# The last expert pair of a mixture-of-experts kernel: down blocks loaded in halves, and unread matrix products between its steps

## Chip, cores and metric

The kernel runs on one core of a Trainium2 chip. The metric is the device time of one execution in microseconds (us), as the median of several runs.

## The reference

Two transformer-like blocks are computed on 512 tokens of width 1024, in float32. The first block ends with an expert layer: 16 experts, each of which picks 64 tokens.

```
cap = EC_CAPACITY * t // N_EXPERTS                     # 2 * 512 // 16 = 64
aff = softmax(einsum('btd,de->bte', h, w_router))
gate, idx = top_k(swapaxes(aff, 1, 2), cap)
xs = h[idx]                                            # 64 tokens for each expert
hid = silu(einsum('becd,edf->becf', xs, w_gate)) * einsum('becd,edf->becf', xs, w_up)
ys = einsum('becf,efd->becd', hid, w_down) * gate
x = x + g2 * zeros.at[idx].add(ys)
```

For one expert w_gate and w_up are 1024x2048 and w_down is 2048x1024, 8 MB each; over 16 experts that is some 400 MB. The second block (attention, convolution, a wide feed-forward layer) works on the result of the first.

## The kernel before

Each engine has its own instruction list, written out by hand, and the lists meet only in semaphores. `sync` is the list of the queue that starts the loads (SP), `tensor` that of TensorE.

The experts are taken in 8 pairs (`p` from 0 to 7). One product computes 64 tokens of the first expert in one half of TensorE's columns, the next product the second expert's in the other half (`o[64 * e:64 * e + 64]`). A pair has 12 steps, 4 for the gate matrices, 4 for the up matrices (`expert_up`, kind 0 and 1) and 4 for the down matrices (the `k` loop from L1219), and each step reads one 2 MB block of each expert. So there are 24 blocks a pair and 192 in all (`NBLK`), number n = 24p + 8 kind + 2k + e for gate and up, 24p + 16 + 2k + e for down. The blocks lie in slots of SBUF that are used in turn; `sync` waits until TensorE has done with what a slot held before, and then starts the load (L565).

A down step has four row groups (`r`), each of four products: two column halves (`f`) by two experts (`e`). In the profile every float32 product is two MATMUL records, so a whole down step is 32 records and half of one is 16. Ahead of its products a step waits for its two blocks (`landed_block`, L1114) and for its transposed hidden values (`hT`). These are made by `turn_h` (L1154): four transposes on TensorE into a bank of PSUM, and a copy out of it by ScalarE (L1592). For pair 7 `turn_h` for steps 0 and 1 stands right behind the up steps, that for steps 2 and 3 in the middle of steps 1 and 2.

For pair 7 the last blocks are loaded in pieces: the blocks of down step 2 (n = 188, 189) as two halves of 1 MB, those of step 3 (n = 190, 191) as a half and two quarters. The first halves of the two experts come first and the later pieces after them, the two experts' in turn. The later pieces have semaphores of their own (`mg`, `mh`, `mq`), for which TensorE waits in front of the row group that reads them (L1225). The blocks of steps 0 and 1 (n = 184 to 187) are whole loads.

Behind the last down step the results are copied out of PSUM (ScalarE and VectorE), `combine` (L1105) adds them into the token rows by a product for each of 8 parts, and the first matrix of the second block is multiplied (L1286 to L1292), one part after each `combine`.

An earlier place of the kernel, the routing, has products whose result nobody reads: `keep_busy` (L1033), each an identity matrix by 256 columns of ones.

Of the kernel before, what the change touches and what calls it, by code (L numbers as in the profile page):

```python
# [17 lines left out]
NEG = -1e30  # L18

DMA_SEMS = (*(f"g{i}" for i in range(6)), *(f"cg{i}" for i in range(4)), *(f"zf{i}" for i in range(4)), "x0", "x1", "rows0", "rows", "small", "ctx", "wple", *(f"scale{i}" for i in range(4)), *(f"shift{i}" for i in range(4)), "w0", "w1", "ptok", "gf", "out",  # L20
            *(f"m{i}" for i in range(9)), "mx", "my", "mz", "rows2", "mg0", "mg1", "mh0", "mh1", "mq0", "mq1")
SEMS = (
    "hi", "lo_v", "pe_gla",
    "pe_pre", "pe_ada", "pe_proj", "pe_scores", "pe_scan", "pe_inter", "pe_fill", "pe_mix", "pe_route", "pe_gather",
# [20 lines left out]
def build_program(nc, I, out):  # L45
    ctx = ExitStack()
    with ctx:
        s = {n: ctx.enter_context(nc.semaphore("s_" + n)) for n in DMA_SEMS + SEMS}
# [5 lines left out]
        def up(ins, name, *key):  # L54
            ins.then_inc(s[name], 1)
            count[name] = at[(name, *key)] = at[name] = count.get(name, 0) + 1
# [19 lines left out]
        banks = [ctx.enter_context(nc.psum_tensor(f"bank{i}", [P, 512], F32)) for i in range(8)]  # L76
# [39 lines left out]
        ident = mem(128)  # L116
        onesD = mem(128)
        onesC = mem(128)
        ones256 = mem(256)
# [60 lines left out]
        NBLK = 192  # L180
# [8 lines left out]
        for n in range(NBLK):  # L189
# [10 lines left out]
            i = SLOT_OF[n] = turn_of[0]  # L200
# [45 lines left out]
        mx, sm = small[:, 96:128], small[:, 144:176]  # L246
# [196 lines left out]
        def sync(sp):  # L443
# [68 lines left out]
            for n in (0, 1, 2, 5, 7, 15, 3, 4, 6, 8, 22, *range(9, 15), *range(16, 22), *range(23, NBLK)):  # L512
                if n == 0:
                    sp.wait_ge(s["pe_inter"], val("pe_inter", 1, 3))
                if n == 1:
                    sp.wait_ge(s["a_fill"], val("a_fill"))
                    sp.wait_ge(s["v_fill"], val("v_fill"))
                    sp.wait_ge(s["g_y"], val("g_y"))
                r, src = n % 24, block(n)
                k = (r - 16) // 2  # L520
                if n == 15:
                    sp.wait_ge(s["pe_mix"], val("pe_mix", "xr", 3, 1))
                    sp.dma_start(once_x, src).then_inc(s["mx"], 16)
                    continue
                if n == 7:
                    sp.wait_ge(s["v_mix"], val("v_mix", "on", 3))
                    sp.dma_start(once_y, src[:, 0:2560]).then_inc(s["my"], 16)
                    continue
                if n == 8:
                    sp.dma_start(once_z, block(7)[:, 2560:3584]).then_inc(s["my"], 16)  # L530
                    sp.dma_start(once_s, block(7)[:, 3584:4096]).then_inc(s["my"], 16)
                if n == 22:
                    sp.wait_ge(s["pe_sq"], val("pe_sq", 1, 7, 0))
                    for place, c0, c1 in ((late_c, 0, 2048), (late_g, 2048, 3584), (late_y, 3584, 4096)):
                        sp.dma_start(place, src[:, c0:c1]).then_inc(s["mz"], 16)
                    continue
                if n in HALVED:
                    for half, z in enumerate((slice(0, 2048), slice(2048, 4096))):
                        for m in HALVES.get(n, ()):
                            used = moe_used(BEFORE[m]) if half else half_used(BEFORE[m])  # L540
                            sp.wait_ge(s[used[0]], val(*used))
                            sp.dma_start(moe_slot[SLOT_OF[m]][:, z], block(m)[:, z]).then_inc(s[f"m{SLOT_OF[m]}"], 16)
                    continue
                if n == 99:
                    sp.wait_ge(s["pe_down"], val("pe_down", 0, 3))
                    for dst, name in ((W2k, "w_cmp_k2_2"), (W2v, "w_cmp_v2_2")):
                        sp.dma_start(dst, I[name][0].rearrange("(k p) n -> p k n", p=P)).then_inc(s["rows2"], 16)
                    used = moe_used(before_ple)
                    sp.wait_ge(s[used[0]], val(*used))
                    sp.dma_start(ptok, I["p_2"][0, 0].rearrange("(t p) d -> p t d", p=P)).then_inc(s["ptok"], 16)  # L550
                    sp.dma_start(ple, I["w_ple_2"][0].rearrange("(k p) n -> p k n", p=P)).then_inc(s["wple"], 16)
                i = SLOT_OF[n]
                if BEFORE[n] is not None:
                    used = moe_used(BEFORE[n])
                    sp.wait_ge(s[used[0]], val(*used))
                elif n == 9:
                    sp.wait_ge(s["pe_route"], val("pe_route", "h2", 3, 1))
                elif n == 3:
                    sp.wait_ge(s["pe_mix"], val("pe_mix", "res", 3))
                elif n == 5:  # L560
                    sp.wait_ge(s["pe_mix"], val("pe_mix", "o", 3))
                elif n == 6:
                    sp.wait_ge(s["pe_mix"], val("pe_mix", "res", 7))
                if n < NBLK - 4:
                    sp.dma_start(moe_slot[i], src).then_inc(s[f"m{i}"], 16)  # L565
                    continue

                sp.dma_start(moe_slot[i][:, 0:2048], src[:, 0:2048]).then_inc(s[f"m{i}"], 16)
                if r % 2:
                    for name, c0, c1 in (("mg", 2048, 4096),) if k == 2 else (("mh", 2048, 3072), ("mq", 3072, 4096)):  # L570
                        for e_ in range(2):
                            src = I["w_down"][0, 14 + e_][512 * k:512 * k + 512, :].rearrange("(p r) n -> p (r n)", p=P)
                            sp.dma_start(moe_slot[SLOT_OF[n - 1 + e_]][:, c0:c1], src[:, c0:c1]).then_inc(s[f"{name}{e_}"], 16)
# [48 lines left out]
        def tensor(pe):  # L622
# [3 lines left out]
            def after(b):  # L626
                if b in free:
                    pe.wait_ge(s[free[b][0]], val(*free[b]))
# [525 lines left out]
            def turn_h(p, fc):  # L1154
                o = take(("hT", p, fc), "hT", p, fc)
                pe.wait_ge(s["v_up"], val("v_up", p, fc))
                up(turn_blocks(o, [ab[:, 512 * fc + 128 * j:512 * fc + 128 * j + 128] for j in range(4)]), "pe_up", "h", p, fc)
# [15 lines left out]
            def ple_product(n):  # L1173
# [6 lines left out]
                                    start=k == 0, stop=k == 1)  # L1180
                up(ins, "pe_ple", "e", n)

            turn["order"], turn["i"] = [6, 7, 4, 5], 0
            gather(0, 0)
            gather(0, 1)
            for p in range(8):
# [14 lines left out]
                for k in range(4):  # L1201
                    if p < 7 and 0 < k < 3:
                        expert_up(p, 1, k, (gather, p + 1, 2 * k - 2))
                        gather(p + 1, 2 * k - 1)
                    else:
                        expert_up(p, 1, k)
                    if p == 5:
                        ple_product(k)
                if 1 < p < 7:
# [9 lines left out]
                for k in range(4):  # L1219
                    ws = [landed_block(24 * p + 16 + 2 * k + e) for e in range(2)]  # L1220
                    pe.wait_ge(s["hT"], val("hT", p, k))
                    for r in range(4):
                        for f in range(2):
                            for e in range(2):
                                if p == 7 and f == 0 and (k, r) in ((2, 2), (3, 2), (3, 3)):  # L1225
                                    pe.wait_ge(s[f"{'mg' if k == 2 else 'mh' if r == 2 else 'mq'}{e}"], 16)
                                ins = pe.matmul(o[f][64 * e:64 * e + 64, :], hT[:, 4 * k + r, 64 * e:64 * e + 64],  # L1227
                                                ws[e](1024 * r + 512 * f), start=k + r == 0, stop=k == 3 and r == 3)
                        if r == 1 and p == 0:
                            up(ins, "pe_half", 2, k)  # L1230
                        if r == 1 and k < 3 and (p < 7 or k):
                            turn_h(p, k + 1)
                    up(ins, "pe_down", p, k)
                    for k_ in later.get(k, ()):
                        gather(p + 1, k_)
                    if p == 4 and k < 2:
                        ple_turned(k)
                    if p == 5:
                        ple_product(4 + k)
                    if p == 1:  # L1240
                        turn_back(2 * k)
                        turn_back(2 * k + 1)
                        combine(0, 2 * k)
                        combine(0, 2 * k + 1)
# [52 lines left out]
            for j in range(4):  # L1297
                if j == 1:
                    for name, row in (("rr", 0), ("r1", 32)):
# [3 lines left out]
                                     start=True, stop=True), "pe_z", name)  # L1303
# [243 lines left out]
            for h in range(2):  # L1547
                os_ = [take(("dn", 4 * h + j), "xt", "dn", 4 * h + j) for j in range(4)]
                for i, (k0, nk) in enumerate(KD):
                    c = DN + 3 * h + i  # L1550
                    wh, wl = tiles(c, nk)
                    for k in range(nk):
                        kk = k0 + k
                        n = 22 * h + kk
# [1594 lines left out]
```

## Time and profile before

| | |
|---|---|
| median of 3 runs | 2057.58 us (2056.42 to 2061.18) |
| profiled execution, its own time | 2058.38 us |
| its span, first to last instruction | 2056.7 us |
| TensorE busy in the span | 1982.4 us, 96% |
| VectorE / ScalarE busy | 889.0 us / 578.2 us |
| DMA, mean over the span | 257 GB/s |
| chain that ended last | TensorE 94%, issue 2%, VectorE 2%, DMA 1%, ScalarE 1% |

The span is less than the execution's own time because what lies before the first and after the last instruction is not in it. Times inside the trace count from the span's start. The granted clock is the share of TensorE's full clock that the chip let through: 1.00 is 2.4 GHz, 0.50 is 1.2 GHz.

### The profile page before, as it was taken

What the parts mean: (1) busy time and instruction counts of PE and PEld (TensorE: products, weight loads), DVE (VectorE), ACT (ScalarE), POOL (GpSimd) and SP (SyncE); (2) the same over time, 40 slices, a digit from 0 to 9 for tenths busy, and PEclk for the clock granted to TensorE, in tenths of its full rate; (3) what the DMA queues carried; (4) which work ended last, traced back from release to release, by engine and by line L of the source; (5) the groups of instructions that cost most, each with busy time, mean ns of one, the idle gap of its engine ahead of it and who ended that gap; (6) DMA issues with size and microseconds to landing.
All of it is one profiled execution on the core that took longest, in us unless ns stands there. A gap on an engine that the chain in (4) does not pass through costs nothing.

```text
span 2056.7 us, 23632 instructions
## 1 busy us (share of the span) xinstructions
PE 1982.4 (96%) x9838; PEld 1232.5 (60%) x9838; DVE 889.0 (43%) x1429; ACT 578.2 (28%) x901; POOL 59.4 (3%) x107
## 2 busy tenths in 40 slices
PE   7999999999999997989999889999999999999998
PEld 5887887443434342333434224776788888888886
DVE  4666673211111020111102002887997556667555
ACT  5434432100000000000000002438635344334445
POOL 0000010000000000000000000006200000000000
PEclk9999999999999999999999999999999999999999
DMA  9462257899999999999999998142222322322322
GB/s 355 164 244 84 79 203 298 370 419 420 429 424 430 431 429 426 431 431 430 427 415 430 431 431 340 64 123 42 72 93 83 112 93 82 118 88 82 113 82 82
DMA packets 115547, 529.58 MB, mean 257 GB/s; under 512 B 15493, under 2 KB 52465, under 8 KB 87921
## 3 DMA queue, kind: packets, MB, share of 16 engines
q1 hardware_dynamic: 115441, 528.07, 63.8%
q8 instruction: 79, 1.29, 0.2%
q14 instruction: 27, 0.22, 0.0%
HBM read 525.95 MB, written 2.10 MB: 257 GB/s over the span
## 4 chain that ended last, share of the span: by engine, by line
PE 94%; issue 2%; DVE 2%; DMA 1%; ACT 1%; ACTq 0%; SPq 0%; DVEq 0%
PE bank L1141 22%; PE bank L665 12%; PE bank L667 12%; PE bank L666 12%; PE bank L1227 11%; PE bank L1095 3%; PE bank L1112 3%; PE bank L686 3%; PE bank L672 3%; PE bank L674 3%; PE bank L676 3%; DMA f<-in_w_down_dram 1%; PE bank L1350 1%; PE bank L1460 1%; PE bank L1179 1%
## 5 line engine op out<-in xcount | busy, mean ns | idle before, releaser
L1141 PE MATMUL bank<-f,high 128*64 128x512 f32 x2048 | 462.7, 599 | 31.7 <-issue 29.9
L665 PE MATMUL bank<-r 128*128 128x512 f32 x912 | 359.4, 394 | 1.5 <-DVE r L2189 1.2
L667 PE MATMUL bank<-r 128*128 128x512 f32 x912 | 355.3, 390 | 0.0
L666 PE MATMUL bank<-r 128*128 128x512 f32 x912 | 355.2, 389 | 0.0
L1141 PEld LDWEIGHTS bank<-f,high 128*64 128x64 f32 x2048 | 146.8, 137 | 317.8 <-issue 313.6
L1227 PE MATMUL bank<-f,high 128*64 128x512 f32 x1024 | 231.8, 600 | 14.3 <-issue 12.6
L2538 DVE SCALAR_TENSOR_TENSOR f<-bank,low,f 128x512 f32<-128x512 f32 x64 | 48.1, 751 | 396.6 <-PE bank L1112 396.1
L1592 ACT ACTIVATE high<-bank 128x512 f32<-128x512 f32 (+2 forms) x97 | 54.6, 580 | 555.7 <-PE bank L686 409.3
L415 DVE TENSOR_TENSOR r<-f,r 128x1024 fp32r<-128x1024 f32 (+2 forms) x167 | 191.1, 1197 | 26.2 <-ACT r L409 26.0
L665 PEld LDWEIGHTS bank<-r 128*128 128x128 f32 x912 | 171.2, 188 | 43.2 <-issue 5.5
L667 PEld LDWEIGHTS bank<-r 128*128 128x128 f32 x912 | 171.2, 188 | 36.2
L666 PEld LDWEIGHTS bank<-r 128*128 128x128 f32 x912 | 171.3, 188 | 35.0 <-issue 0.5
L409 ACT ACTIVATE r<-f 128x1024 fp32r<-128x1024 f32 (+2 forms) x168 | 161.4, 1027 | 28.6 <-DMA f<-in_w_in_dram 9.8
L1227 PEld LDWEIGHTS bank<-f,high 128*64 128x64 f32 x1024 | 72.6, 137 | 147.6 <-issue 146.5
L2524 DVE TENSOR_SCALAR high<-bank,low 128x128 f32<-128x128 f32 x64 | 25.8, 408 | 247.2 <-PE bank L1095 246.6
L1820 ACT ACTIVATE high<-bank 128x512 f32<-128x512 f32 x32 | 16.5, 602 | 294.3 <-PE bank L1141 294.3
L1095 PEld LDWEIGHTS bank<-high 128*128 128x128 f32 x512 | 63.6, 196 | 28.7 <-issue 28.7
L2659 DVE SCALAR_TENSOR_TENSOR f<-high,low,f 128x511 f32<-128x511 f32 (+29 forms) x120 | 80.0, 735 | 0.1
L665 PE MATMUL bank<-r,r 128*128 128x512 f32 (+1 forms) x208 | 75.0, 361 | 0.0
L667 PE MATMUL bank<-r,r 128*128 128x512 f32 (+1 forms) x208 | 74.2, 357 | 0.0
L666 PE MATMUL bank<-r,r 128*128 128x512 f32 (+1 forms) x208 | 74.2, 357 | 0.0
L686 PEld LDWEIGHTS bank<-low,high 128*128 128x128 f32 x430 | 48.6, 145 | 37.9 <-issue 32.0
(415 smaller groups left out, 2041.9 us busy)
## 6 DMA issues: line engine op xcount, KB each, us to landing
f<-in_w_up_dram SPq DMA_DIRECT2D x58, 2048.0 KB, 17.1
f<-in_w_down_dram SPq DMA_DIRECT2D x56, 2048.0 KB, 20.2
f<-in_w_gate_dram SPq DMA_DIRECT2D x55, 2048.0 KB, 17.4
f<-in_w_up_dram SPq DMA_DIRECT2D x34, 1024.0 KB, 7.2
f<-in_w_in_dram SPq DMA_DIRECT2D x13, 2048.0 KB, 7.7
f<-in_w_down_dram SPq DMA_DIRECT2D x21, 1024.0 KB, 10.1
high<-in_w_ada_dram SPq DMA_DIRECT2D x32, 512.0 KB, 6.0
f<-in_w_gate_dram SPq DMA_DIRECT2D x16, 1024.0 KB, 9.3
```

Source lines behind the costliest of these rows:

```text
L409: up(a.activation(high_part(c)[:, z], whole(c)[:, z], ACT.Copy), "hi", c, i)
L415: up(v.tensor_tensor(low_part(c)[:, z], whole(c)[:, z], high_part(c)[:, z].bitcast(F32), ALU.subtract), "lo_v", c, i)
L665: pe.matmul(o, wh, xh, start=first, stop=False)
L666: pe.matmul(o, wl, xh, start=False, stop=False)
L667: return pe.matmul(o, wh, xl, start=False, stop=last)
L672: pe.matmul(o, w, xh, start=first, stop=False)
L674: pe.matmul(o, w, xh, start=False, stop=False)
L686: ins = pe.transpose(o[:, m * n:m * n + m] if k == P else o[:, k * n:k * n + k], b, ident[0:k, 0:k])
L1095: ins = pe.matmul(o, H2[:, t, 256 * (k // 2) + k % 2:256 * (k // 2) + 256:2], Sp[i][:, t, :], start=t == 0, stop=t == 3)
L1141: ins = pe.matmul(o[64 * e:64 * e + 64, :], xsT[p % 2][:, 2 * k + r, 64 * e:64 * e + 64], ws[e](2048 * r + 512 * fc), start=k == 0 and r = ...
L1227: ins = pe.matmul(o[f][64 * e:64 * e + 64, :], hT[:, 4 * k + r, 64 * e:64 * e + 64], ws[e](1024 * r + 512 * f), start=k + r == 0, stop=k = ...
L2659: ins = v.scalar_tensor_tensor(out=CO[:, j, s_:], in0=CI[:, j, :T - s_], scalar=cw2[:, k:k + 1], in1=CO[:, j, s_:], op0=ALU.mult, op1=ALU.add)
```

## The change

In `sync` the bound for whole loads moves from `NBLK - 4` to `NBLK - 6`, so that the two blocks of pair 7's down step 1 (n = 186, 187) are loaded as two halves each as well, first half of one expert, first half of the other, then the two second halves with new semaphores `mf0` and `mf1`. In `tensor` a wait for these stands in front of row group 2 of that step. A new function `fill_in(b, n)` issues n unread products into bank b. It is called with three products behind each of pair 7's four up steps (12 in all, bank 3), and in its down steps with four products behind step 0, two in the middle and two at the end of steps 1 and 2 (12 in all, bank 7). Where one stands in the middle of a step it comes right behind `turn_h`.

```diff
-                if n < NBLK - 4:
+                if n < NBLK - 6:
                     sp.dma_start(moe_slot[i], src).then_inc(s[f"m{i}"], 16)
                     continue
 
                 sp.dma_start(moe_slot[i][:, 0:2048], src[:, 0:2048]).then_inc(s[f"m{i}"], 16)
                 if r % 2:
-                    for name, c0, c1 in (("mg", 2048, 4096),) if k == 2 else (("mh", 2048, 3072), ("mq", 3072, 4096)):
+                    for name, c0, c1 in (("mf" if k == 1 else "mg", 2048, 4096),) if k < 3 else (("mh", 2048, 3072), ("mq", 3072, 4096)):
...
+            def fill_in(b, n):
+
+                after(b)
+                for _ in range(n):
+                    pe.matmul(banks[b][:, 0:256], ident, ones256, start=True, stop=True)
+
...
                     else:
                         expert_up(p, 1, k)
+                    if p == 7:
+                        fill_in(3, 3)
...
-                                if p == 7 and f == 0 and (k, r) in ((2, 2), (3, 2), (3, 3)):
-                                    pe.wait_ge(s[f"{'mg' if k == 2 else 'mh' if r == 2 else 'mq'}{e}"], 16)
+                                if p == 7 and f == 0 and (k, r) in ((1, 2), (2, 2), (3, 2), (3, 3)):
+                                    pe.wait_ge(s[f"{'mf' if k == 1 else 'mg' if k == 2 else 'mh' if r == 2 else 'mq'}{e}"], 16)
...
                         if r == 1 and k < 3 and (p < 7 or k):
                             turn_h(p, k + 1)
+                        if p == 7 and (r == 1 and 0 < k < 3 or r == 3 and k < 3):
+                            fill_in(7, 2 if k else 4)
```

## Rows read from the trace of the kernel before

**Rows 1.** Windows: busy us of each engine, granted clock, DMA share, GB/s.
```profile
1240.00:1260.00 20.00, 17.48 (x76) 6.29 (x74) 0.00 (x0) 0.60 (x1) 0.00 (x0) 0.91 1.00 425
...
1340.00:1360.00 20.00, 20.00 (x91) 16.41 (x90) 18.49 (x53) 5.91 (x10) 0.00 (x0) 1.00 0.48 106
```

**Rows 2.** Chain of waits through pair 7: start us, us, what.
```profile
1206.67 2.68 issue
...
1238.64 7.09 PE bank L1227 x32
1245.73 2.52 issue
1248.25 5.35 PE bank L1227 x16
1253.60 0.59 PE bank L686 x4
1254.18 7.02 PE bank L1227 x32
1261.20 0.59 PE bank L686 x4
1261.79 10.47 PE bank L1227 x48
...
1272.82 2.81 PE bank L1112 x6
```

**Rows 3.** Loads of pair 7's down blocks: start us of issue, then time to landing.
```profile
L565 SPq DMA_DIRECT2D f<-in_w_down_dram x1: 328/328/328, 1226.2 to 1226.2; - x1
DMA to landing us min/median/max: 22.0/22.0/22.0
...
L573 SPq DMA_DIRECT2D f<-in_w_down_dram x1: 441/441/441, 1236.8 to 1236.8; - x1
DMA to landing us min/median/max: 21.2/21.2/21.2
...
L568 SPq DMA_DIRECT2D f<-in_w_down_dram x1: 328/328/328, 1245.8 to 1245.8; - x1
DMA to landing us min/median/max: 17.1/17.1/17.1
...
L573 SPq DMA_DIRECT2D f<-in_w_down_dram x2: 432/433/434, 1247.1 to 1247.6; - x2
DMA to landing us min/median/max: 19.5/19.9/20.3
```

**Rows 4.** Windows of 1 us and 10 us, columns as in Rows 1.
```profile
1249.00:1250.00 1.00, 1.00 (x6) 0.42 (x4) 0.00 (x0) 0.00 (x0) 0.00 (x0) 0.50 1.03 434
...
350.00:360.00 10.00, 9.78 (x56) 8.15 (x54) 8.01 (x21) 3.81 (x8) 0.00 (x0) 1.00 0.98 401
```

**Rows 5.** Timeline of TensorE around idle times in an earlier pair's gate and up steps.
```profile
817.03 6.05 PE L1141 MATMUL bank<-f,high 128*64 128x512 f32 x16 [4.64 <-issue]
...
857.48 3.65 PE L1141 MATMUL bank<-f,high 128*64 128x512 f32 x16 [3.12 <-issue]
```

**Rows 6.** Timeline of TensorE in the routing: ten unread products and what follows.
```profile
353.21 4.48 PE L1036 MATMUL bank<-low 128*128 128x256 f32 x20
357.52 0.38 PE L1045 MATMUL bank<-low,f 128*128 128x128 f32 x2
```

**Rows 7.** Chain of waits: a `combine` between half-array products, and one between full-array products.
```profile
1193.56 1.06 PE bank L1112 x2
...
1278.58 0.86 PE bank L1112 x2
```

**Rows 8.** Timelines of ScalarE and VectorE beside pair 7's up and down steps.
```profile
1198.25 2.06 ACT L1820 ACTIVATE high<-bank 128x512 f32<-128x512 f32 x4 [39.03 <-PE bank L1141]
...
1236.58 1.08 ACT L1592 ACTIVATE high<-bank 128x512 f32<-128x512 f32 x2 [36.27 <-PE bank L686]
...
1233.41 3.77 DVE L2572 TENSOR_TENSOR high<-bank,high 128x512 f32<-128x512 f32 x4 [33.37 <-PE bank L1141]
```

More of the change, by code:

```diff
@@ L20 @@
 DMA_SEMS = (*(f"g{i}" for i in range(6)), *(f"cg{i}" for i in range(4)), *(f"zf{i}" for i in range(4)), "x0", "x1", "rows0", "rows", "small", "ctx", "wple", *(f"scale{i}" for i in range(4)), *(f"shift{i}" for i in range(4)), "w0", "w1", "ptok", "gf", "out",
-            *(f"m{i}" for i in range(9)), "mx", "my", "mz", "rows2", "mg0", "mg1", "mh0", "mh1", "mq0", "mq1")
+            *(f"m{i}" for i in range(9)), "mx", "my", "mz", "rows2", "mf0", "mf1", "mg0", "mg1", "mh0", "mh1", "mq0", "mq1")
 SEMS = (
```

## The prediction

> **What bounds the kernel now.** First the windows around the end of the expert layer [rows 1]. From 1240 to 1260 the DMA engines are full (share 1.00, 425 GB/s), TensorE is busy 17.48 of 20 us, and the granted clock is 0.91. From 1340 on it is the other way round: TensorE is busy 20.00 of 20 us and the DMA moves a quarter of that. So pair 7 is where the kernel passes from being bound by loads to being bound by TensorE, and what TensorE is late by when it leaves pair 7 stays to the end.
>
> Next the chain of waits through pair 7 [rows 2]. Each up step ends with TensorE idle for some 2.7 us (one such row stands there). Down step 0 starts at 1238.64 and takes 7.09 us. Then come 2.52 us of idle time, until the second block of step 1 has landed: issued 1226.2, landed 22.0 us later, 1248.2 [rows 3]. From 1248.25 on TensorE runs through to 1261.79 + 10.47 = 1272.26 without a wait, although the last pieces land late: the second halves of step 2 at 1236.8 + 21.2 = 1258.0, the first halves of step 3 at 1245.8 + 17.1 = 1262.9, its last quarter at 1247.6 + 20.3 = 1267.9. In that stretch the first half of step 1 took 5.35 us. Two row groups cost 7.02 / 2 = 3.51 us elsewhere in the chain, so 1.84 us were lost there, and the windows say to what: the granted clock was 0.50 [rows 4], 1.2 GHz. The engine had been idle for 2.52 us just before.
>
> So between 1238.64 and 1272.26 there are 33.62 us: four steps of 7.02 (28.1), two `turn_h` of 0.59 (1.2), 2.52 of waiting, 1.84 of low clock.
>
> **The change part by part.**
>
> *Halves of step 1.* They can remove at most the wait of 2.52 us. Four megabytes land in 1258.0 − 1248.2 = 9.8 us [rows 3], already in 1 MB halves, so 2.45 us for each half. The order of step 1 becomes first, first, second, second, the last of them at 1248.2 as before, and the two first halves are there at 1248.2 − 4.9 = 1243.3, before step 0 ends. The wait goes: −2.52. On SP there are two more loads to start, 0.43 us each [rows 3], in front of step 2's first half; that one is queued for over 20 us before it lands, so this is hidden. One second half is issued some 10 us later than it would be as part of a whole block, and still 19 us before it is due. Cost 0; bounds −0.1 and +0.9 us on the landings, and there are 4 us of slack for that (below).
>
> *The clock.* With no idle time behind step 0 I expect no fall: −1.84. Bounds 0 and −1.84. An earlier idle time of 4.64 us was also followed by slow products (6.05 for 3.65 us), but one of 3.12 us was not [rows 5]; so the length of one gap doesn't decide, and 2.52 is nearer to the case that was spared. I take the full gain, because in the new order the engine isn't idle at all from 1238.7 on. The Trainium skill ("TensorE: Matmul & The Clock Gate", Part 1) says that the moment at which the chip judges activity runs free of the kernel, so that the same kernel meets a different number of slow products from run to run. Rows 5 agree with that. By it the fall at 1248 need not be in each run of the kernel before; this is a rival below.
>
> *Unread products in the down steps.* Ten of them in a row took 357.52 − 353.21 = 4.31 us, 0.431 each [rows 6]. Twelve are 5.17 us. A change from half-array to full-array products and back costs something too: a `combine` between half-array products takes 1.06 us, between full-array ones 0.86 [rows 7], a difference of 0.20. Behind `turn_h`, which is itself full-array, nothing is added; three groups stand alone (end of steps 0, 1, 2): 0.6 us, bounds 0 and 0.6. What hides them? Only waits could, and in the new order there are none left. Running the list forward from 1238.7: step 0 ends 1245.8, four products 1247.7, step 1's first half 1251.2, `turn_h` and two products 1252.7, second half 1256.2, two products 1257.2, step 2's first half 1260.7, then 1262.2, second half 1265.7, 1266.8, step 3 to 1273.8. The data that each part needs landed at 1243.3, 1248.2, 1253.1, 1258.0, 1262.9, and step 3's last quarter at 1267.9 for use at 1272.0. Each is some 4 us ahead. So TensorE never waits, and the whole 5.17 + 0.6 = 5.8 us stand on the path. Taken alone the other way: without products the list would be held at 1258.0, 1262.9 and the end would be about 1270.2; there are only some 2.3 us of waits to fill, and 5.8 us go in.
>
> *Unread products in the up steps.* Three are 1.3 us, plus up to 0.2 for the change of array use, in idle times of 2.7 us [rows 2]; behind the first three steps they are covered and cost nothing. The clock is full there already, so they gain nothing either. Behind the last one they push `turn_h` and the copy by ScalarE back by 1.3 us. The copy now runs from 1236.58, two in 1.08 us [rows 8]; moved to 1237.9, the first is done at 1238.5. With some 0.2 us from engine to engine for the way from ScalarE to TensorE (an estimate: 1272.82 − 1272.26 = 0.56 us hold a copy and two such ways) [rows 2] that is 1238.7, against 1238.64: +0.1. Bounds 0 (if the load stays the later one) and +1.3.
>
> *Waits for the banks.* Bank 3 is free when ScalarE has read the gate values, 1198.25 + 2.06 = 1200.3, before its first use at 1206.7. Bank 7 is free after VectorE's last product, 1233.41 + 3.77 = 1237.2, before its first use at 1245.8 [rows 8]. Cost 0.
>
> **Sum:** −2.52 − 1.84 + 5.17 + 0.6 + 0.1 = +1.5 us. The down steps end at 1273.8 instead of 1272.3. What follows is `combine` at 1272.82 and then TensorE without idle time [rows 1, 2], so nothing takes the 1.5 us up. The profiled execution has 2058.38 us (span 2056.7 and 1.7 around it); it would have 2059.9. The median of the runs is 0.8 lower, 2057.58, and so 2059.1 is forecast. What a measurement of this kernel can tell from no change is about 0.2%, 4.1 us: the forecast is "no measurable change, if anything slower".
>
> **Rivals.**
>
> 1. *The low clock is not in most runs of before.* For it: the 3.12 us gap without a fall [rows 5], and a median 0.8 us below the profiled time. Against it: where a gap and low clock are both shown, I have one execution only. Then 1.84 us aren't there to win: +3.3, 2060.9.
>
> 2. *The products hide in waits.* If the halves of step 1 to 3 came later than reckoned (1 MB pieces in another order on the same full queue), TensorE would be idle between its parts and the products would be free. For it: the DMA share of 1.00 up to 1260 [rows 1]. Against: 4 us of slack in all these places, and the end is then set by the last quarter and cannot lie before 1267.9 + 0.2 + 1.8 = 1269.9. The best this can give is −2.1: 2055.5.
>
> 3. *Slower: the products don't hold the clock.* Place: 1245.8 to 1273.8. If unread products of 256 columns count for less than the products of the steps, the chip lowers the clock in this stretch although TensorE never rests. Each microsecond at 1.2 GHz costs half a microsecond; to get from +1.5 to the 4.1 us that can be told, it must last over 5.2 us, longer than the 4.8 us behind the 4.64 us gap (6.05 − 3.65 = 2.4 lost, twice that in low clock) [rows 5]. Over the whole 28 us it would be +14: 2073. For it: the clock fell in this very place. Against: in the routing, where such products fill the time between short transposes, the granted clock is 1.00 [rows 4].
>
> 4. *The change doesn't do what it says* in the up steps: the clock is 1.00 there and stays so. That is part of the forecast already and is worth 0.
>
> **How the numbers follow.** Forecast (+0.5 to +2.5) 0.60; rival 1 (+2.5 to +4.1) 0.18; rival 2 (0.5 to −2.1) 0.14; rival 3 0.04; 0.04 for what I don't see. The likeliest is +1.5, 2059.1. The three runs of before differ by 4.8 us, so a median of a few runs is good to about a microsecond. The range takes in the forecast, rival 1 to its price and the upper half of rival 2: 2056.3 to 2061.7. Faster by over 0.2% would take more than the 2.1 us that are in all waits of pair 7's end: 0.03. Slower: rival 3 and the upper edge of rival 1: 0.05. Within: 0.92.
>
> **What would show it.** In the profile after: down step 1 starts at about 1247.7, with no idle time between 1238.7 and 1273.8; granted clock 1.00 from 1240 to 1274; groups of unread products of 0.43 us each, three with 0.2 us of change before or after; the last down product ends at 1273.8; the loads land as before. The forecast fails if TensorE shows idle time in front of a product group, if the down steps end before 1272, or if the clock is under 1.00 in any window there. It also fails if a later part takes the 1.5 us up.

## The result, and the profile after

The changed kernel takes 2059.15 us, the kernel before 2056.59 us (medians of 20 runs each). The ratio is 1.0014, with a 95% interval of 1.0008 to 1.0020: slower by 0.14%, some 1.6 to 4.1 us. Timed a second time the ratio was 1.0014 (1.0005 to 1.0023). The change does not pay; it costs a little, less than the 0.2% below which the forecast had spoken of no change. The median that the forecast named, 2059.1, is met to 0.1 us, but that is luck: it stood on three runs of before (2057.58), which lay 1.0 us above the median of twenty, and the difference added to it, 1.5 us, was 1.1 us too small.

The two profiled executions hide this, 2058.43 us after and 2058.38 before, with the same span of 2056.7. The loads of the one after were ahead when pair 7 came: its first up step starts at 1197.85, that of before at 1199.58. So the stretch has to be measured from a common point, not from the ends.

The chain of waits of the changed kernel through pair 7's up and down steps (start us, us, what; L1235 are the down products, L1187 the unread ones):
```profile
1197.85 7.09 PE bank L1141 x32
1204.94 1.49 PE bank L1187 x6
1206.43 1.09 issue
...
1234.07 1.49 PE bank L1187 x6
1235.56 0.45 PE bank L686 x4
...
1236.09 0.61 ACT high L1602
...
1236.90 7.09 PE bank L1235 x32
1243.99 1.92 PE bank L1187 x8
1245.91 3.58 PE bank L1235 x16
1249.50 0.59 PE bank L686 x4
1250.09 0.87 PE bank L1187 x4
1250.95 3.58 PE bank L1235 x16
1254.54 1.06 PE bank L1187 x4
1255.60 3.58 PE bank L1235 x16
...
1264.22 1.06 PE bank L1187 x4
1265.28 7.04 PE bank L1235 x32
...
1272.88 2.81 PE bank L1112 x6
```
Beside [rows 2] two things are gone: the idle 2.52 us in front of step 1, and the 5.35 us for its first half, now 3.58. In their place stand five groups of L1187, 1.92 + 0.87 + 1.06 and two more of the last two kinds, 5.78 us. The stretch from the start of down step 0 to the end of the last down product is 1265.28 + 7.04 − 1236.90 = 35.42 us, against 33.62 before: +1.80. From the start of the first up step it is 74.47 against 72.68: +1.79. What follows, the `combine` of 2.81 us, is as it was.

Windows of the changed kernel (columns as in [rows 1]):
```profile
1240.00:1260.00 20.00, 20.00 (x94) 8.54 (x91) 0.00 (x0) 0.79 (x2) 0.00 (x0) 1.00 1.01 424
...
1340.00:1360.00 20.00, 20.00 (x91) 16.37 (x91) 18.49 (x53) 5.91 (x10) 0.00 (x0) 1.00 0.47 105
1235.00:1273.00 38.00, 36.95 (x172) 15.26 (x171) 1.01 (x2) 2.94 (x7) 0.00 (x0) 1.00 1.02 419
```
From 1240 to 1260 TensorE is now busy all the time and its clock is full, as it is in all of the down steps (1235 to 1273); before it was 17.48 us at 0.91. That 2.52 us more of "busy" bought nothing: the wait is filled up with work that nobody reads. Busy time in this window rose and so did the run time. From 1340 to 1360 TensorE is busy all the time, as before.

Loads of the changed kernel (start of issue, time to landing):
```profile
L568 SPq DMA_DIRECT2D f<-in_w_down_dram x1: 328/328/328, 1224.4 to 1224.4; - x1
DMA to landing us min/median/max: 17.1/17.1/17.1
...
L573 SPq DMA_DIRECT2D f<-in_w_down_dram x2: 432/433/434, 1224.8 to 1225.3; - x2
DMA to landing us min/median/max: 19.2/20.2/21.2
...
L568 SPq DMA_DIRECT2D f<-in_w_down_dram x1: 327/327/327, 1244.0 to 1244.0; - x1
DMA to landing us min/median/max: 17.1/17.1/17.1
```
The later first half of step 1 lands at 1241.5, its later second half at 1225.3 + 21.2 = 1246.5, step 3's first halves at 1261.1. TensorE uses them at 1245.91, 1250.95 and 1265.28. The halves of step 2 land at 1251.3 and 1256.2, for use at 1255.60 and 1260.63. Each is more than 4 us early, so no product of the five groups lies in a wait.

### The profile page after: what moved, and what is told of

Read it like the earlier page. It is cut to its first block, busy times and chain, and to the rows that moved or that the text cites. A ratio compares the mean times of both kernels' runs of the same rounds, so it can differ in the third digit from the quotient of the medians.

```text
span 2056.7 us, 23730 instructions
## 1 busy us (share of the span) xinstructions
PE 1995.5 (97%) x9886; PEld 1239.1 (60%) x9886; DVE 888.8 (43%) x1429; ACT 577.7 (28%) x901; POOL 59.1 (3%) x107
## 4 chain that ended last, share of the span: by engine, by line
PE 95%; issue 2%; DVE 1%; ACT 1%; DMA 0%; ACTq 0%; SPq 0%
PE bank L1141 22%; PE bank L665 12%; PE bank L666 12%; PE bank L667 12%; PE bank L1235 11%; PE bank L1095 3%; PE bank L1112 3%; PE bank L686 3%; PE bank L672 3%; PE bank L674 3%; PE bank L676 3%; PE bank L1360 1%; PE bank L1470 1%; PE bank L1179 1%; PE bank L1187 1%
## 5 line engine op out<-in xcount | busy, mean ns | idle before, releaser
L665 PE MATMUL bank<-r 128*128 128x512 f32 x912 | 359.5, 394 | 1.5 <-DVE r L2199 1.2
L1235 PE MATMUL bank<-f,high 128*64 128x512 f32 x1024 | 230.6, 597 | 10.5 <-issue 10.1
L665 PEld LDWEIGHTS bank<-r 128*128 128x128 f32 x912 | 171.2, 188 | 43.3 <-issue 5.5
L1235 PEld LDWEIGHTS bank<-f,high 128*64 128x64 f32 x1024 | 71.6, 137 | 142.3 <-issue 141.2
L665 PE MATMUL bank<-r,r 128*128 128x512 f32 (+1 forms) x208 | 75.1, 361 | 0.0
L1095 PE MATMUL bank<-high 128*128 128x128 f32 x512 | 71.0, 289 | 0.0
```

Of the source, the lines that this page charges most:

```text
L665: pe.matmul(o, wh, xh, start=first, stop=False)
L1095: ins = pe.matmul(o, H2[:, t, 256 * (k // 2) + k % 2:256 * (k // 2) + 256:2], Sp[i][:, t, :], start=t == 0, stop=t == 3)
```

## The experiments

Theory A is the forecast's: the unread products of the down steps stand on TensorE's path, and halves and clock give less back than they cost. Where a stretch is given, it runs from the start of down step 0 to the end of the last down product; "since the up steps" is the same end counted from the start of pair 7's first up step, which the loads pace.

| kernel | stretch, us | since the up steps, us | median, us (before, timed beside it) | ratio |
|---|---|---|---|---|
| before, as first profiled | 33.62 | 72.68 | 2056.59 | |
| changed | 35.42 | 74.47 | 2059.15 (2056.59) | 1.0014 (1.0008 to 1.0020) |
| halves only | 31.53 | 70.59 | 2055.08 (2056.75) | 0.9991 (0.9982 to 1.0000) |
| halves, up products | 29.69 | 71.86 | 2055.15 (2056.75) | 0.9993 (0.9984 to 1.0001) |
| down products, whole blocks | 35.72 | 75.08 | 2059.88 (2056.75) | 1.0015 (1.0006 to 1.0024) |
| changed, down products doubled | 40.60 | 79.65 | 2063.99 (2056.75) | 1.0036 (1.0024 to 1.0049) |
| before with four products | 31.86 | 70.92 | 2055.57 (2056.64) | 0.9999 (0.9990 to 1.0008) |
| before, profiled again (3) | 31.5 each | 70.9 each | one run each | |
| changed, again | 35.4 | 74.3 | 2058.97 (2056.46) | 1.0014 (1.0005 to 1.0023) |
| halves only, again | 31.45 | 70.5 | 2054.59 (2056.46) | 0.9993 (0.9985 to 1.0002) |
| halves, three products in waits | 31.3 | 70.6 | 2055.25 (2056.46) | 0.9993 (0.9984 to 1.0002) |

**Halves alone.** Both calls of `fill_in` are taken out of the changed kernel.
```diff
-                    if p == 7:
-                        fill_in(3, 3)
...
-                        if p == 7 and (r == 1 and 0 < k < 3 or r == 3 and k < 3):
-                            fill_in(7, 2 if k else 4)
```


> Both groups of unread products are left out, the loads in halves and the new wait stay. Theory A (the products of the down steps stand on TensorE's path, 5.8 us of them, and the halves and the clock give 4.4 back): from the start of down step 0 to the end of the last down product 31.5 us, against 33.62 before and 35.42 in the changed kernel; idle time of about 0.8 us before the second half of step 2 and 1.4 us before step 3; the execution 2 us (0.1%) faster than before, 4 us faster than the changed kernel. Rival B (the halves themselves cost: two more 1 MB loads in another order make the blocks land later): step 1's second half lands more than 1 us after where the whole blocks did, the stretch is 33.6 us or more and the execution is no faster than before.

The chain of waits of this kernel (L1233 are the down products):
```profile
1214.15 21.97 DMA f<-in_w_down_dram
...
1236.36 10.52 PE bank L1233 x48
1246.88 0.59 PE bank L686 x4
1247.47 7.10 PE bank L1233 x32
1254.57 0.59 PE bank L686 x4
1255.16 4.26 PE bank L1233 x16
1259.42 1.37 issue
1260.79 7.10 PE bank L1233 x32
...
1268.44 2.81 PE bank L1112 x6
```
The stretch is 31.53 us, as theory A had it. Down step 0 and the first half of step 1 run without a gap (x48 in 10.52). The wait has moved: 1.37 us in front of step 3, and 4.26 − 3.51 = 0.75 inside step 2's second half. So of the 2.52 us of wait taken away in front of step 1, 2.1 come back as waits further on, because the loads still end when they end. The gain over before is 1.7 us by the medians, with an interval that ends at no change. Rival B asked for a stretch of 33.6 us or more and falls: the halves cost nothing.

**Halves and the products of the up steps.** Only the second call is taken out.
```diff
-                        if p == 7 and (r == 1 and 0 < k < 3 or r == 3 and k < 3):
-                            fill_in(7, 2 if k else 4)
```


> Halves and the twelve unread products behind the up steps; those of the down steps are left out. Theory A: the up products lie in idle time, so the stretch of the down steps is 31.5 us as with the halves alone and the execution within 0.5 us of it, 2 us faster than before; down step 0 starts 0.1 to 0.3 us later after its data has landed than before. Rival C (the three products behind the last up step hold back the transposes and so down step 0): 1.3 us or more slower than the halves alone.

The median is within 0.1 us of the halves alone: no cost or gain of the up products shows. Single runs of one kernel differ by more than the 1.3 us of rival C, so this alone does not settle it; the changed kernel does, whose step 0 starts 0.3 us behind its block with these products in place. The stretch was a miss, 29.69 us and not 31.5, and down step 0 started 2.0 us behind its load (1237.4 and 1239.36), not 0.1 to 0.3 us later than before. In this execution the last up step ran at a low clock in spite of the products (8.78 us for 7.09, in the timeline below). Its block came late, 11.23 us after the start of the step before it instead of 9.7, so that TensorE was idle for 2.65 us behind the products and not for 1.1. The down steps then started late, found more of their loads landed, and had only 0.29 us left to wait in front of step 3. Since the up steps they ended 1.3 us later than the halves alone (71.86 and 70.59), about what that block was late by.
```profile
1216.58 7.09 PE L1141 MATMUL bank<-f,high 128*64 128x512 f32 x32 [1.11 <-issue]
1223.59 1.56 PE L1187 MATMUL bank<-low 128*128 128x256 f32 x6
1227.81 8.78 PE L1141 MATMUL bank<-f,high 128*64 128x512 f32 x32 [2.65 <-issue]
...
1261.95 7.09 PE L1235 MATMUL bank<-f,high 128*64 128x512 f32 x32 [0.29 <-issue]
```

**The products of the down steps alone**, on the kernel before with its whole blocks.
```diff
+                        if p == 7 and (r == 1 and 0 < k < 3 or r == 3 and k < 3):
+                            fill_in(7, 2 if k else 4)
```


> Loads as before (step 1 in whole blocks), with the twelve unread products of the down steps and none behind the up steps. Theory A: the first four (1.9 us) lie in the 2.5 us wait in front of step 1, the other eight are 3.9 us on the path, a full clock in step 1 gives 1.84 back: the stretch of the down steps is 35.7 us, the execution 2 us slower than before. Rival D (the products are hidden and the cost of the change lies in the halves): the stretch is 31.8 us and the execution 1.8 us faster than before.

Stretch 35.72 us (35.7 forecast); ratio 1.0015, 3.1 us by the medians (2 forecast). The first four products lie in the wait in front of step 1, of which 0.23 us is left; the other eight stand on the path. The price of the change is here, with no half of step 1 in the kernel. Rival D falls.

**Twice the products.**
```diff
-                            fill_in(7, 2 if k else 4)
+                            fill_in(7, 4 if k else 8)
```


> The changed kernel with 24 unread products in the down steps instead of 12 (8 behind step 0, 4 at each of the other four places). Theory A: each is 0.431 us on the path: the stretch of the down steps is 35.4 + 5.2 = 40.6 us, the execution 5.2 us slower than the changed kernel, some 8 us (0.4%) slower than before. Rival D (they lie in waits for the blocks): the stretch grows by less than 2 us.

The chain of waits of this kernel:
```profile
1240.95 7.09 PE bank L1235 x32
1248.04 3.65 PE bank L1187 x16
1251.69 3.58 PE bank L1235 x16
...
1274.51 7.04 PE bank L1235 x32
```
The stretch is 40.60 us, 5.18 more than with twelve, 0.432 for each product. The median is 4.8 us above the changed kernel's first one, 2059.15, where 5.2 was expected, and 7.2 above before. In the chain each product stands on the path at its full price; the price read from [rows 6], 0.431, had it right.

**Four products in the wait of before.** Loads as before; only the group behind down step 0.
```diff
+                        if p == 7 and r == 3 and k == 0:
+                            fill_in(7, 4)
```


> The kernel before with only four unread products behind down step 0 (1.9 us, inside its wait of 2.5 us), loads in whole blocks. Theory F (the moment of a clock fall runs free of the kernel, so it hits the down steps in some executions only): the stretch of the down steps is 31.8 us when the clock is full and the execution 0 to 1 us faster than before. Rival G (the 2.5 us wait in front of step 1 brings the clock down in every execution, and the products keep it up): 1.8 us faster than before.

Stretch 31.86 us with a full clock, ratio 0.9999 (0.9990 to 1.0008). By the medians that is 1.1 us of gain, by the ratio 0.2. Rival G's 1.8 us lie inside the interval, at its edge (0.9991 against 0.9990), so the times alone don't exclude it.

**The kernel before, profiled three times more.**

> The kernel before, profiled once more. Theory F: the granted clock falls in another step than down step 1, or in none of pair 7; if the down steps have a full clock, their stretch is 31.8 us. Rival G: down step 1's first half takes 5.0 to 5.4 us again and the stretch 33.6 us.

> The kernel before, profiled a third time; what each theory expects is as for the second profile: F a fall in another place or none, stretch 31.8 us; G the fall in down step 1, stretch 33.6 us.

> The kernel before, profiled a fourth time; what each theory expects is as for the second profile: F a fall in another place or none, stretch 31.8 us; G the fall in down step 1, stretch 33.6 us.

The timeline of TensorE in the first of the three; in the other two every duration is the same to 0.1 us:
```profile
1207.99 8.70 PE L1141 MATMUL bank<-f,high 128*64 128x512 f32 x32 [2.65 <-issue]
1217.70 7.09 PE L1141 MATMUL bank<-f,high 128*64 128x512 f32 x32 [1.01 <-issue]
1227.44 8.78 PE L1141 MATMUL bank<-f,high 128*64 128x512 f32 x32 [2.65 <-issue]
...
1237.64 7.09 PE L1227 MATMUL bank<-f,high 128*64 128x512 f32 x32 [0.40 <-DVE high L2572]
1246.89 3.65 PE L1227 MATMUL bank<-f,high 128*64 128x512 f32 x16 [2.15 <-issue]
...
1258.66 10.52 PE L1227 MATMUL bank<-f,high 128*64 128x512 f32 x48
```
None of the three has the low clock in down step 1: its first half takes 3.65 us after an idle time of 2.15. In all three the clock fell in the second and the fourth up step instead (8.70 and 8.78 us for 7.09). There the idle time that follows shrinks from 2.65 to 1.01 and takes the loss up; the fall in the fourth step only lets down step 0 start on VectorE's result instead of on its load. The stretch is 31.5 us. Theory F had expected 31.8; its main point stands, and G falls as a rule for each execution: the fall of [rows 4] was in one profile of four.

**The changed kernel and the halves, once more.**

> The changed kernel, timed and profiled once more beside the others of this call. Theory A with theory F: down step 0 to the end of the last down product takes 35.4 us again with a full clock and no idle time; against an execution of before with a full clock in the down steps (31.5 us, a start 0.3 to 1.3 us later) it is 3.6 us slower, against one with a fall there 1.8 us; the median 1.8 to 3.6 us slower than before.

> Halves alone once more. Theory A with theory F: the stretch is 31.5 us and ends 31.8 us after step 0's blocks have landed, against 32.1 us in an execution of before without a fall and 33.9 us in one with it: the median 0.3 to 2.1 us faster than before, 3.5 us faster than the changed kernel. Rival H (the halves gain their whole 2.5 us of wait): 2.5 us faster than before or more.

The stretches repeat to 0.1 us (35.4 and 31.45). Changed against before is 1.0014 again, 2.5 us by the medians, between the 1.8 and 3.6 that were expected; halves 0.9993, so rival H (2.5 us or more) is not borne out by the medians (1.9). The interval (0.9985 to 1.0002) includes both rival H and no change; against H stand the chains, in which 2.1 us of wait come back.

**Three products, placed in waits.** Halves, nothing behind the up steps, and:
```diff
+                        if p == 7 and k == 2 and r in (1, 3):
+                            fill_in(7, 1 if r == 1 else 2)
```


> Halves, no products behind the up steps, and in the down steps only three unread products at the two places where the halves alone left TensorE idle: one in the middle of step 2 (0.4 us, idle 0.75 us) and two at its end (1.1 us, idle 1.4 us). Theory A: products that lie in a wait are free; the stretch is 31.5 to 31.8 us and the execution within 0.5 us of the halves alone. Rival (each product costs its 0.43 us wherever it stands): 1.3 us or more slower than the halves alone.

The chain of waits of this kernel:
```profile
1256.84 0.43 PE bank L1187 x2
1257.27 3.71 PE bank L1233 x16
1260.98 1.06 PE bank L1187 x4
1262.04 0.30 issue
```
A little wait is still left behind the last group (0.30 us), the stretch is 31.3 us, and the median is 0.2 to 0.7 us above the two of the halves alone, with the same ratio of 0.9993. So three products that lie in a wait cost nothing that shows here, where twelve on the path cost 0.43 us each.

The fastest of these kernels is the halves alone, 1.7 and 1.9 us below before by the medians, with intervals that just reach no change. Against the changed kernel it is 4 us.

## Why the prediction was right, and where its size was off

*Products of the down steps, +5.8 us, no wait left to hide them.* Right: 5.78 us in five groups, the loads 4 us ahead at each place, and 0.432 us for each product when they were doubled. The 0.2 us for the change of array use shows in the groups (1.06 where one stands alone, 0.87 behind `turn_h`).

*Halves, −2.52 us.* Right as a term in this sum, because the products use up what the halves free. That they cost nothing on the landings is right too: step 1's last half lands 9.9 us behind step 0's last block (1246.5 and 1236.6), its whole block before 9.8 (1248.2 and 1238.4). On their own the halves give far less: 2.1 of the 2.5 us return as waits for the next blocks. Against a profile of before without the fall 0.3 us are left (70.6 and 70.9 since the up steps), so most of the 1.7 and 1.9 us of the medians would have to come from executions with the fall; that was not measured.

*Up products, 0.* Right in time, wrong in its reason. "The clock is full there already" held for the one profile that was read. In the nine profiles without these products 12 of 36 up steps of pair 7 took 8.5 to 8.8 us instead of 7.09; in the four with them 1 of 16 did, the one with 2.65 us of idle time in front of it. So it looks as if the products hold the clock up, though 16 steps are few. It is worth nothing, since a slow up step ends inside the wait for its next block.

*The clock in the down steps, −1.84 us.* This is the term that was mis-sized. The sum took the whole of it from one profile; the fall was in one of four profiles of before. Without it the stretch of before is 31.5 us, and the changed kernel is 74.4 − 70.9 = 3.5 us slower since the up steps; with it 1.8. The measured 2.6 us (ratio 1.0014, 2.9 us) lie between, above the forecast's 1.5 and under rival 1's 3.3. Rival 1 was no alternative to the forecast but a part of it: the two cases come in different executions of the same kernel. About half of the executions with a fall would fit the medians (an estimate), but the share in timed runs was not measured, so it stays open how the 2.6 us are made up.

The Trainium skill ("TensorE: Matmul & The Clock Gate", Part 1) says that the chip's watch over TensorE's activity runs free of the kernel's start, so that the moment of a clock change varies from run to run. The four profiles of before agree: the fall stood in down step 1 once and in two up steps three times. Three of them are alike, but other kernels with the same up steps had it elsewhere: the halves alone in the third step only, the three products in waits in the fourth only. The rows that the prediction called in agreement, [rows 5], come from one execution and can't show a difference between runs.

*The stretch as a whole* was forecast as 1273.8 − 1238.7 = 35.1 us and measured as 35.4. The 0.3 us are in the products of the steps themselves: behind each of the first four groups a half step took 3.58 instead of 3.51 us, and step 3 took 7.04 instead of 7.02. That the steps did not end at 1273.8 but at 1272.32 is due to the earlier start, 1236.90 for 1238.7. Down step 0 did start on ScalarE's copy, as reckoned, 0.3 us behind its load (1236.6), against 0.25 before: the 1.3 us by which the up products push the copy back cost nothing to speak of.

*Rival 2* (products hidden in waits) fell by the chain; its own sum does not close, since an end at 1269.9 would be 2.4 us early and not 2.1. *Rival 3* (they don't hold the clock) fell by the window 1235 to 1273 at 1.00.

## What to carry to other kernels

Add up the waits that will be left after an edit, not those that are there now: halves that free 2.5 us at one step and filler of 5.8 us leave the engine later than it was, and the filler must fit what remains. Filler that may keep a clock up is worth its price only where no wait behind a slow step would take it up anyway, and here it was free only inside a wait. Before a clock loss of 2 us is booked as a gain, profile the same kernel several times: it may sit elsewhere in the next execution.

## What the runs showed of the hardware

TensorE's clock fell in some steps of a steady pattern, 7.1 us of products and 2.6 us of idle time, and not in others; the granted clock over the slow step was 0.81 in the second profile of before:
```profile
1227.40:1236.20 8.80, 8.76 (x33) 3.21 (x33) 2.46 (x3) 0.00 (x0) 0.00 (x0) 0.81 1.00 426
```
In those steps the next wait took the loss up; where TensorE bounds the path, as in the down steps, the loss stayed: before took 72.68 us since the up steps with the fall there, and 70.9 without. The profiled execution of the kernel with doubled products took 2067.6 us, 3.6 above that kernel's median. It alone of the thirteen profiles has a low clock here, far ahead of pair 7, behind an idle time of 1.53 us in the first block:
```profile
190.00:200.00 10.00, 9.40 (x94) 8.54 (x96) 2.89 (x8) 0.60 (x1) 0.00 (x0) 0.66 0.22 83
```
In the other twelve this window reads 1.00, with an idle time of 1.53 or 1.54 us at the same place, so the gap alone does not bring the fall. From the end of the gap to the next block of products (L665) it is 12.06 us here and 8.96 us in the first profile of before: 3.1 us are lost, most of the distance to the median.
